# Group B of the attention: one 256-column matmul per key block that two steps share, where there were two of 128

## The reference

```python
def mixer_b(q, k, v, rel_table):
    ...
    logits = jnp.einsum('bcqhd,bckhd->bhcqk', qc.astype(jnp.float32),
                        kb.astype(jnp.float32)) * SCALE
    ...
    logits = logits + bias[:, None]
    valid = band_valid(nc, B_BAND)
    logits = jnp.where(valid[:, None, :], logits, NEG)
    p = jax.nn.softmax(logits, axis=-1)
    out = jnp.einsum('bhcqk,bckhd->bcqhd', p.astype(vb.dtype), vb)
    return out.reshape(b, s, B_W)

def reference(...):
    ...
        h = rmsnorm(x, g_pre_mix[l])
        proj = jnp.einsum('bsd,de->bse', h, w_in[l]) + b_in[l]
        ...
        mix = jnp.concatenate([out_a, out_b], axis=-1)
        y = jnp.einsum('bse,ed->bsd', mix, w_out[l])
        x = x + rmsnorm(y, g_post_mix[l])
        h = rmsnorm(x, g_pre_mlp[l])
        u = jnp.square(jax.nn.relu(jnp.einsum('bsd,df->bsf', h, w_up[l])))
        y = jnp.einsum('bsf,fd->bsd', u, w_down[l])
        x = x + rmsnorm(y, g_post_mlp[l])
```

## Time and profile before

| | |
|---|---|
| median of 3 runs | 1046.79 us (1046.38 to 1046.83) |
| the profiled execution | 1046.1 us, of which the span of the trace is 1044.3 us |
| PE busy | 1035.4 us, 99% of the span |
| DVE / ACT / POOL busy | 761.4 / 473.9 / 213.8 us |
| steps 32 to 53 (group B with `fill`) | about 185 to 297 us of the span |
| steps 54 to 63 | about 297 to 335 us |

### The profile page before, as it was taken

How to read it: one execution, slowest core, us unless ns; L and a number is a source line. 1 busy time by engine, 2 the same in 40 slices (tenths; PEclk the granted TensorE clock), 3 DMA queues, 4 the chain that set the end, 5 groups by cost and what they waited for, 6 DMA issues and landing times.

```text
span 1044.3 us, 15928 instructions
## 1 busy us (share of the span) xinstructions
PE 1035.4 (99%) x5631; PEld 861.7 (83%) x5631; DVE 761.4 (73%) x1509; ACT 473.9 (45%) x972; POOL 213.8 (20%) x200
## 2 busy tenths in 40 slices
PE   9999999999999999999999999999999999999997
PEld 8899888788777888888888888888888888888886
DVE  5853477767679457879988878776444777788997
ACT  6533256545469457855222131131344444444562
POOL 0400000000000002139767476573100000000000
PEclk9999999999999999999999999999999999999999
DMA  9460110111052123134543444446777733454344
GB/s 253 109 211 12 47 52 35 47 50 38 26 159 105 61 96 116 52 101 182 207 176 136 151 157 160 139 156 212 239 244 246 240 99 99 133 190 147 98 139 164
DMA packets 81742, 137.95 MB, mean 132 GB/s; under 512 B 16744, under 2 KB 34032, under 8 KB 79616
## 3 DMA queue, kind: packets, MB, share of 16 engines
q1 hardware_dynamic: 80976, 136.75, 40.1%
q10 hardware_dynamic: 688, 0.20, 0.1%
HBM read 98.67 MB, written 42.51 MB: 135 GB/s over the span
## 4 chain that ended last, share of the span: by engine, by line
PE 95%; DVE 2%; issue 1%; ACT 1%; DMA 0%; DVEq 0%; SPq 0%; ACTq 0%
PE ps L2027 27%; PE ps L2029 27%; PE ps L2028 27%; PE ps L2236 2%; PE ps L2222 2%; PE ps L2203 2%; PE ps L2151 1%; PE ps L2182 1%; PE ps L2343 1%; PE ps L2357 1%; PE ps L2355 1%; PE ps L2164 1%; PE ps L2373 1%; PE ps L2039 1%; DMA xraw<-in_x 0%
## 5 line engine op out<-in xcount | busy, mean ns | idle before, releaser
L2027 PE MATMUL ps<-b_hi,wc_hi 128*128 128x512 f32 x448 | 174.9, 390 | 0.0
L2029 PE MATMUL ps<-tm_hi,sm_lo 128*128 128x512 f32 (+1 forms) x450 | 174.8, 388 | 0.0
L2028 PE MATMUL ps<-tm_lo,sm_hi 128*128 128x512 f32 (+1 forms) x450 | 174.8, 388 | 0.0
L2027 PE MATMUL ps<-tm_hi,sm_hi 128*128 128x512 f32 (+1 forms) x450 | 174.8, 388 | 0.0
L2029 PE MATMUL ps<-b_hi,wc_lo 128*128 128x512 f32 x448 | 174.5, 390 | 0.0
L2028 PE MATMUL ps<-b_lo,wc_hi 128*128 128x512 f32 x448 | 174.5, 390 | 0.0
L1336 ACT ACTIVATE sm_hi<-sm_raw 128x512 fp32r<-128x512 f32 x112 | 70.7, 631 | 161.8 <-DMA sm_raw<-u_matrices 161.7
L1936 DVE TENSOR_TENSOR sm_lo<-sm_raw,sm_hi 128x512 fp32r<-128x512 f32 x112 | 77.7, 694 | 77.7 <-ACT sm_hi L1336 76.6
L2027 PEld LDWEIGHTS ps<-b_hi,wc_hi 128*128 128x128 f32 x448 | 84.1, 188 | 18.2 <-DVE wc_lo L1723 0.6
L2029 PEld LDWEIGHTS ps<-tm_hi,sm_lo 128*128 128x128 f32 x450 | 84.5, 188 | 17.5
L2028 PEld LDWEIGHTS ps<-tm_lo,sm_hi 128*128 128x128 f32 x450 | 84.5, 188 | 17.4
(11 more groups left out here) (232 smaller groups left out, 2078.9 us busy)
## 6 DMA issues: line engine op xcount, KB each, us to landing
u_matrices<-stage SPq DMA_DIRECT2D x112, 256.0 KB, 2.0
sm_raw<-u_matrices SPq DMA_DIRECT2D x112, 256.0 KB, 2.6
up_raw<-in_w_up SPq DMA_DIRECT2D x16, 1024.0 KB, 5.0
w<-in_w_down SPq DMA_DIRECT2D x64, 256.0 KB, 3.6
w_raw<-in_w_in SPq DMA_DIRECT2D x8, 512.0 KB, 3.4
xr<-in_x SPq DMA_DIRECT2D x8, 512.0 KB, 3.5
x_rows<-xr SPq DMA_DIRECT2D x8, 512.0 KB, 2.6
xf<-x_rows SPq DMA_DIRECT2D x8, 512.0 KB, 3.6
```

Of the source, the lines that this page charges most:

```text
L2027: pe.matmul(out, w_hi_, x_hi_, start=start, stop=False)
L2028: pe.matmul(out, w_hi_, x_lo_, start=False, stop=False)
L2029: return pe.matmul(out, w_lo_, x_hi_, start=False, stop=stop)
```

## The change

`weigh_two(n)` takes the place of `weigh(n)` and `weigh(n + 1)` in the loop above, for n = 32, 34, ... 50: ten pairs of steps. A key block that both steps look at is weighed by one matmul for each head, whose 256 moving columns are that block of step n and that block of step n + 1 (two runs of 128, in the two slots of `probT_b`), and whose result goes to two neighbouring tiles of bank 7. Blocks that only one of the two steps looks at keep a matmul of 128 columns. `s_pv` is raised by two at the end, and both steps' copies are waited for ahead of the first matmul.

```diff
+            def weigh_two(n):
+                p, t = n // T, n % T
+                begins = [t + 1 - keys_of(n), t + 2 - keys_of(n + 1)]
+                pe.wait_ge(s_pta, copies(n + 1, True))
+                pe.wait_ge(s_ptd, copies(n + 1, False))
+                if n % 4 == 0:
+                    pe.wait_ge(s_mix, n // 4 + 1)
+                at = P + P * (p - 4)
+                out_ = ps[:, 7, (t % 4) * P:(t % 4) * P + 2 * P]
+                wide = probT_b[:].rearrange("p s n -> p (s n)")
+                runs = ([(j, 0, 2) for j in range(begins[1], t + 1)] + [(j, 0, 1) for j in range(begins[0], begins[1])]
+                        + [(t + 1, 1, 2)])
+                for i, (j, s0, s1) in enumerate(runs):
+                    for hh in range(2):
+                        rows = slice(64 * hh, 64 * hh + 64)
+                        block = [(2 * s + hh) * B_KEYS * P + (j - begins[s]) * P for s in range(2)]
+                        first = wide[:, block[s0]:block[s0] + P]
+                        moving = first if s1 - s0 == 1 else bass.AP(
+                            first.tensor, first.offset, [list(first.ap[0]), [block[1] - block[0], 2], [1, P]])
+                        last = pe.matmul(out_[rows, s0 * P:s1 * P], v_tok[:, j, at + 64 * hh:at + 64 * hh + 64], moving,
+                                         start=(i == 0), stop=(i == len(runs) - 1))
+                last.then_inc(s_pv, 2)
+
...
                 if A_STEPS + 2 < n < LATE and n % 2:
-                    weigh(n - 3)
-                    weigh(n - 2)
+                    weigh_two(n - 3)
```

## The result

The changed kernel takes 1049.03 us (median of 11 runs, 1048.65 to 1049.63), the kernel before 1046.83 us (median of 11 runs beside them). The ratio is 1.0022, 95% interval 1.0014 to 1.0030: 2.2 us slower. The prediction was 1049.4 us, slower, in a range of 1047.3 to 1050.3 us.

The account below looks back on a forecast made before the run. The prediction took PE, busy 99% of the span, to bound the kernel. It added 2.20 + 0.34 + 0.22 us of waits less 0.19 us saved to 1046.79 us: 1049.4 us, range 1047.3 to 1050.3 us.

Parts of the forecast that it names:

- PE is the bound, and a stall counts in full: Whole span: PE is busy 99% and 95% of the chain, so every stretch in which it stands still counts.
- Joined wait, pairs 38/39 and 46/47: Twenty records of the first step no longer cover the wait for ACT's late copy: +1.10 us twice, +2.20 us.
- Pairs 36/37 and 44/45: At these pairs' start PE waits for DVE's copy of the last chunk: 0.08 to 0.17 us each, +0.34 us taken.
- Pair 32/33: Four records that ran ahead of the wait for DVE's copy now come behind it: +0.22 us.
- The wide matmul: In the ten pairs, moving columns set the pace, so 56 wide matmuls save only 0.19 us.
- Rival 1: Weight loads set the pace of `weigh`: 6.2 us saved against 2.76 us of waiting, 1043.4 us; chance 0.08.
- Rival 2: DVE and ACT clear their queues while PE stands, shortening later waits by about 2 us: 1047.4 us; chance 0.08.
- Rival 3: After PE stands 1.15 and 1.32 us the clock falls to 1.2 GHz: near 1052.5 us; chance 0.04.
- Rival 4: Wide matmuls with two runs of columns no longer run side by side: +12.3 us more, 1061.7 us; chance 0.02.
- The sum: All terms over the ten pairs: 2.20 + 0.34 + 0.22 - 0.19 = +2.57 us, added to the median 1046.79 us.
- the likeliest case: Forecast time with bounds for DVE's copies, columns, rounding and measurement: 1048.7 to 1050.2 us; chance 0.78.

Follow-up runs that it names:

- the wait alone: Kernel before with narrow matmuls kept; only the copies of both steps are waited for ahead of the first step: 1049.17 us, ratio 1.0021.
- two fills first: Changed kernel with two of the four fill products of the same pass moved ahead of pairs 38/39 and 46/47: 1046.61 us, ratio 0.9996.
- half the columns: Kernel before, matmuls of steps 32 to 51 moving 64 columns instead of 128 with the same weight loads: 1040.60 us, ratio 0.9941.
- one head: Kernel before, steps 32 to 51 weighing head 0 only, the matmuls of head 1 left out: 1046.75 us, ratio 1.0003.
- heads apart by step: Kernel before, in each of steps 32 to 51 all key blocks of one head, then all of the other: 1052.38 us, ratio 1.0052.
- heads apart over the pair: Kernel before, matmuls of a pair of steps ordered by head, head 0 of both steps, then head 1: 1058.37 us, ratio 1.0110.

## Why the prediction was right, step by step

- **PE is the bound, and a stall counts in full.** Right. PE's lateness of 2.53 us at 276 us is, within 0.1 us, the 2.6 us by which the span ends later.
- **Joined wait, pairs 38/39 and 46/47, +1.10 us each.** Right: the lateness grew by 1.09 us at the first and by 1.08 at the second (1.45 us behind pair 44/45, 2.53 behind 46/47). The waits read 1.08 and 1.24 us, released by ACT's L1019 as foreseen; by starts PE stood 1.17 and 1.32 us, since the row counts only from the modelled end of the matmul before. Of that 0.05 and 0.22 us were paid before too. The kernel with the wait alone shows that this is the cause, and the one with two fills first that it can be undone.
- **Pairs 36/37 and 44/45, +0.17 us each.** Over-sized: 0.11 us each. PE began pair 36/37 0.31 us later than before, and 0.20 of that stood already behind pair 34/35 (205.11 against 204.91). It began pair 44/45 1.47 us later, and 1.36 of that stood ahead of the pair. PE went on 0.11 us after the copy's end (214.88 + 0.41 to 215.40) and 0.10 us at the other pair, between the prediction's bounds of 0.06 and 0.15, of which it took the upper. That makes the sum 0.12 us too high.
- **Pair 32/33, +0.22 us.** Right for the four records: the row behind is 0.81 us after 194.16, where it was 0.59. But both kernels go on at 194.16, though PE was 0.06 us late in the changed one: there it followed DVE's copy by 0.09 us, before by 0.15. The pair itself added 0.16 us, which the prediction could not have read from the rows it had.
- **The wide matmul, -0.19 us.** Right in kind and near in size: 0.14 us over the ten pairs, 0.02 us in each pair of 28 or 40 records and nothing that can be read in those of 12. Moving columns were taken as the pace, which half the columns and one head show.
- **Rival 1, loads as the pace**, is ruled out: forty loads fit in 1.32 us. On the two rules weighed there: "FP8 and Floating Point Precision" of the Trainium skill, TensorE precision notes, has four passes for true FP32, by estimate 213 ns for 128 columns; two records of 0.109 us, 0.218 us for a matmul alone, agree with it. "TensorE: Matmul & The Clock Gate" of the Trainium skill, section on LDWEIGHTS, gives a load by its formula, by estimate 53 ns for 64 columns; that can stand only if the loads of the two heads overlap, since a pair of records with its two loads came in under 0.06 us at half the columns. "TensorEngine Tiling (Array Packing)" of the Trainium skill, key properties, says that different tiles can execute their loads in parallel; the pair of 0.06 us agrees, and no run here shows a load by itself.
- **Rival 2, the stall given back**, did not happen: behind pair 46/47 PE was 2.53 us late, and behind pair 50/51 it was 2.53 still (295.14 against 292.61). **Rival 3, a lower clock**: the clock of the stretch reads 1.00, and the 24 records behind 1.24 us of standing took 2.31 us, the same as in the kernel with two fills first, where PE had not stood. **Rival 4, no side by side with two runs of columns**: ruled out by the same 2.32 us.
- **The sum.** It gave +2.57 us; the stretch of the change measured +2.47 in the trace, and the runs +2.2, with an interval of 1.5 to 3.1. So the runs confirm the direction and the size of the main term, and only the trace tests terms of a tenth or two. There the errors are small and partly cancel: DVE's copies 0.12 us and pair 32/33 0.06 us too high, the saving 0.05 us too large. The two profiled executions differ by 2.9 us (1049.03 against 1046.1), their spans by 2.6; single executions of one kernel differ by as much as the 0.4 us between that and the runs. The upper end of the likeliest case is added wrongly: the bounds named for it give 1050.4 us and not 1050.2. The result lies far from it.

## What to carry to other kernels

Joining two pieces of work joins their waits too: price what the first piece covered, and move other work ahead of the joined wait. Before a matmul is widened to save instructions, look in the trace at what one costs per column: where the moving columns are the pace, as here, half as many matmuls of twice the columns cost nearly the same. A wait that ends about when its cover ends is hardly seen in the trace of before: here it was 0.05 and 0.22 us between two starts, in no row of the waits, and that is where the loss stood.

## What the runs showed of the hardware beyond that

Two matmuls of 64 weight columns on different halves of the array's columns cost together what one costs alone: leaving out 140 of 280 records changed the time by 0.03 us, and twenty records of one head took 2.33 us where forty of both took 2.34. It holds in full only when the halves alternate. With runs of ten records on one half the change of half still won 0.38 us, 3.5 records, and with runs of twenty it won 0.37 us: a piece that doesn't grow with the run. (With runs of six and eight, pair 34/35 of heads apart by step, it was 0.34 us on average: 28 x 0.109 + 0.14 - 2.16, over three changes.)

The starts of the single records show where the piece comes from. With heads apart over the pair, the first seventeen records of pair 36/37 stand 0.109 us apart (the first two 0.160), the seventeenth at 218.785. The next starts 0.006 us behind it, at 218.791, and has the modelled length of 0.32 us that the pair's first record has too, where the others have 0.27. From there two trains are interleaved, each 0.109 us apart: one ends with its twentieth record at 219.113, the other goes on to its twentieth. With heads apart by step it is the same at the seventh record of ten (216.782 and 216.788). In pairs 34/35 and 40/41 of heads apart over the pair, with runs of fourteen and six, the other head begins 0.006 us behind the eleventh and the third (205.139 and 243.486). So the other head's first record starts while three of the first head's are still to start, in runs of 6, 10, 14 and 20. The records do not name the head; that a record starts out of turn is read from the spacing, since in the kernel with one head no two starts are less than 0.109 us apart. What sets the number three, no run here shows.
